# A blocked diagonal scan by quarters, its chunk ends carried in two levels, and output products split by local and entering states

## What is computed

```python
xr = jnp.einsum('btgc,gpc->btgp', uf, bb_re)
xi = jnp.einsum('btgc,gpc->btgp', uf, bb_im)
...
sr, si = complex_scan(jnp.broadcast_to(ar, xr.shape), jnp.broadcast_to(ai, xr.shape), xr, xi)
y = (jnp.einsum('btgp,gcp->btgc', sr, cmat_re) - jnp.einsum('btgp,gcp->btgc', si, cmat_im) + d_skip * uf)
...
mix = (y @ w_glu_v) * jax.nn.sigmoid(y @ w_glu_g)
```

## Time and profile before

| | |
|---|---|
| Median of 3 runs | 2838.79 us (2837.02 to 2840.55) |
| Profiled execution, its own time | 2840.19 us |
| Its span | 2838.5 us |
| TensorE busy | 2742.9 us, 97% |
| VectorE, ScalarE, POOL busy | 1603.1, 1163.9, 388.4 us |
| Mean granted clock | 0.982 of full |

### The profile page before, as it was taken

How to read it: one execution, slowest core, us unless ns; L and a number is a source line. 1 busy time by engine, 2 the same in 40 slices (tenths; PEclk the granted TensorE clock), 3 DMA queues, 4 the chain that set the end, 5 groups by cost and what they waited for, 6 DMA issues and landing times. The chain is left out here.

```text
span 2838.5 us, 53109 instructions
## 1 busy us (share of the span) xinstructions
PE 2742.9 (97%) x19433; PEld 2701.6 (95%) x19433; DVE 1603.1 (56%) x2651; ACT 1163.9 (41%) x1501; POOL 388.4 (14%) x508
## 2 busy tenths in 40 slices
PE   8999999999999999999999993999999999999997
PEld 7999999999999999999999983999999999999996
DVE  7656666555554455655555557665554555455554
ACT  5444445333433333435553332544433344334432
POOL 1333333221000000060002450210000000000011
PEclk9999999999999999999999997999999999999998
DMA  6444444456554545445444420545555554555543
GB/s 176 121 129 122 128 135 123 122 141 156 142 142 141 144 142 146 134 135 147 140 135 136 135 84 5 141 132 154 148 143 150 151 148 142 146 154 149 145 138 95
DMA packets 739209, 382.91 MB, mean 135 GB/s; under 512 B 13560, under 2 KB 734756, under 8 KB 739140
## 3 DMA queue, kind: packets, MB, share of 16 engines
q1 hardware_dynamic: 722352, 365.34, 45.4%
q10 hardware_dynamic: 14228, 9.31, 1.1%
q0 software_dynamic: 2560, 7.29, 1.0%
HBM read 373.31 MB, written 8.57 MB: 135 GB/s over the span
## 5 line engine op out<-in xcount | busy, mean ns | idle before, releaser
L973 DVE TENSOR_TENSOR wl<-raw,wh 128x1024 fp32r<-128x1024 f32 x708 | 894.3, 1264 | 925.4 <-ACT wh L477 924.8
L1499 PE MATMUL banks<-h,wh 128*128 128x336 f32 (+1 forms) x3648 | 1164.6, 319 | 9.2 <-DVE h L983 3.6
L1500 PE MATMUL banks<-h,wh 128*128 128x336 f32 (+1 forms) x3648 | 1152.1, 316 | 0.0
L1501 PE MATMUL banks<-h,wl 128*128 128x336 f32 (+1 forms) x3648 | 1149.7, 315 | 0.0
L477 ACT ACTIVATE wh<-raw 128x1024 fp32r<-128x1024 f32 x708 | 748.8, 1058 | 941.8 <-PE banks L1501 928.4
L1499 PEld LDWEIGHTS banks<-h,wh 128*128 128x128 f32 x3648 | 689.6, 189 | 14.0 <-issue 4.1
L1500 PEld LDWEIGHTS banks<-h,wh 128*128 128x128 f32 x3648 | 689.1, 189 | 3.3 <-issue 1.7
L1501 PEld LDWEIGHTS banks<-h,wl 128*128 128x128 f32 x3648 | 688.6, 189 | 0.0
L1499 PE MATMUL banks<-act,wh 128*128 128x336 f32 (+1 forms) x1888 | 598.6, 317 | 8.6 <-DVE GA L1073 3.2
L1500 PE MATMUL banks<-act,wh 128*128 128x336 f32 (+1 forms) x1888 | 594.7, 315 | 0.0
L1501 PE MATMUL banks<-act,wl 128*128 128x336 f32 (+1 forms) x1888 | 592.8, 314 | 0.0
(11 more groups left out here) (341 smaller groups left out, 1728.3 us busy)
## 6 DMA issues: line engine op xcount, KB each, us to landing
raw<-in_w_up SPq DMA_DIRECT2D x172, 512.0 KB, 4.0
raw<-in_w_gate SPq DMA_DIRECT2D x172, 512.0 KB, 3.9
raw<-in_w_down SPq DMA_DIRECT2D x160, 448.0 KB, 3.6
raw<-in_w_in_e SPq DMA_DIRECT2D x96, 512.0 KB, 3.8
raw<-in_w_out_e SPq DMA_DIRECT2D x32, 512.0 KB, 3.8
raw<-in_w_down SPq DMA_DIRECT2D x32, 512.0 KB, 3.8
raw<-in_w_in_c SPq DMA_DIRECT2D x16, 512.0 KB, 4.1
raw<-in_w_glu_v SPq DMA_DIRECT2D x16, 512.0 KB, 3.8
```

Source lines behind the costliest of these rows:

```text
L973: v.tensor_tensor(wl[:, j % RING, :], raw[:, j % RING, :], wh[:, j % RING, :].bitcast(F32), ALU.subtract) \
L1499: pe.matmul(out, whi, hi, start=first and k == 0, stop=False)
L1500: pe.matmul(out, whi, lo, start=False, stop=False)
L1501: ins = pe.matmul(out, wlo, hi, start=False, stop=last and k == kn - 1)
```

## The change

POOL makes `CT3` before the scan, in what was the table `BX`, and for `CT4` only the zeros; VectorE makes `CT4`. ScalarE takes all eight X products. The scan goes by quarters. The chunk ends are carried within four groups of four chunks at once, then from group to group with the 64th power (`A64`), and a fix-up adds what enters each group, into a tile `SCt` with the chunks innermost. The spread no longer adds into `xs` but writes a ring `sp5`; the output products are made twice, of the local states (75 columns, as quarters are scanned) and of what enters (64 columns). The final states are turned behind the fourth `glu` body. The core of the diff:

```diff
@@ -58,10 +58,10 @@
 CREDIT = 4
...
-POWERS = (1, 2, 3, 4, 8, 12, 16)
+POWERS = (1, 2, 3, 4, 8, 12, 16, 32, 48)
 
 
 COL = {}
...
-            for j in (0, 2, 4, 5, 6, 7):
+            for j in range(8):
                 e.wait_ge(x5, j + 1)
                 take_x(lambda to, x: sc.activation(to, x, ACT.Copy), j).then_inc(x5a, 1)
-            e.wait_ge(scan5, 2)
+            e.wait_ge(scan5, 4)
             sc.activation(fin5[:, 1:1 + NS].rearrange("p s r q -> p r q s"), xs[:, :, :, XW - NS:XW], ACT.Copy)
+            e.wait_ge(quarters, 1)
+            sc.activation(SCt[:, :, :, 0:PCH:4], SC[:, 0:PCH:4].rearrange("p c r q -> p r q c"), ACT.Copy).then_inc(fourth, 1)
+            sc.activation(fin5[:, 0], SC[:, PCH - 1], ACT.Copy).then_inc(fin_made, 1)
...
-                              ACT.Copy).then_inc(ends5, 1)
+                sc.activation(sp5[:, u % SPREAD_RING, :, :, 3, :], SCt[:, :, q, 0:CH], ACT.Copy).then_inc(ends5, 1)
+
+            for u in range(SPREAD_RING):
+                ends(u)
...
+            ph = PH["glu"]
+
+            def glu(i):
+                for j in range(4):
...
+            with e.Fori(0, 4) as i:
+                glu(i)
             for s in range(9):
                 e.wait_ge(fs_t, s + 1)
                 sc.activation(io5o[:, s, :], BM[s % 2][0:2 * PAIRS, 0:P], ACT.Copy).then_inc(fs_c, 1)
...
+            e.wait_ge(out_dma, 16 * (STORES_A + STORES_F + STORES_C))
             ffn(1, None)
...
+            for n, (a5, b5) in enumerate(((0, 0), (1, 0), (1, 1), (3, 3), (4, 3), (4, 4), (6, 6), (7, 6))):
+                pole_product(at(n + 1), at(a5), at(b5))
+            pole_product((A64[:, 1], A64[:, 2]), at(7), at(7))
...
+            e.wait_ge(bx_used, STEP)
+            e.wait_ge(ms_done, 3)
+            for j0 in (0, 4):
+                first, second = (t[:, 0:16 * C5].rearrange("p (q c) -> p q c", c=C5) for t in (sq, ssq))
+                for r in range(2):
+                    times_power(gp, st, C0, 2, r, first, second, OF_C, j0, j0 + 4)
+                    st.then(into_blocks(gp, first, second, CT3[:, j0:j0 + 4, r, :]))
+            gp.memset(sq[:, 0:1], 0.0).then_inc(ct_made, 1)
             e.wait_ge(evac, PH["glu"].group(0, 0) + BANK_CREDIT)
-            gp.tensor_copy(xs[:, :, :, BLK + 1 + PCH:2 * BLK], st5.rearrange("p s r q -> p r q s")).then_inc(st_in, 1)
...
-            for n, to in ((3, CT3), (4, CT4)):
-                gp.memset(to[:], 0.0)
-                for r in range(2):
-                    times_power(gp, st, C0, n - 1, r, cpq[:, r, 0], cpq[:, r, 1], to)
-                for r in range(2):
-                    ins = into_blocks(gp, r, cpq[:, r, 0], cpq[:, r, 1], to)
-                ins.then_inc(ct_made, 1)
-                e.wait_ge(ct_made, n - 2)
+            gp.tensor_copy(xs[:, :, :, BLK + PCH:2 * BLK], st5.rearrange("p s r q -> p r q s")).then_inc(st_in, 1)
+            gp.memset(CT4[:], 0.0).then_inc(ct4_zero, 1)
...
-            e.wait_ge(out_dma, 16 * (STORES_A + STORES_F + STORES_C))
...
+            e.wait_ge(ap_made, 1)
+            for r in range(2):
+                times_power(v, st, C0, 3, r, cpq[:, r, 0], cpq[:, r, 1], OF_C)
+            e.wait_ge(ct4_zero, 1)
+            for r in range(2):
+                ins = into_blocks(v, cpq[:, r, 0], cpq[:, r, 1], CT4[:, :, r, :])
+            ins.then_inc(ct4_made, 1)
...
-            for j in (1, 3):
-                e.wait_ge(x5, j + 1)
-                take_x(v.tensor_copy, j).then_inc(x5v, 1)
...
-            def scan_half(half):
-
...
+
+                v.tensor_tensor(prod0, re, prev, ALU.mult)
+                st.then(v.tensor_tensor(prod1[:, ::-1], ims[:, ::-1], prev, ALU.mult))
+                st.then(v.tensor_tensor(prod0, prod0, prod1, ALU.add))
+
+            def scan_quarter(u):
+
+                q = slice(u * QUARTER, (u + 1) * QUARTER)
+                e.wait_ge(x5a, 2 * u + 2)
                 for i in range(1, 4):
                     n = PCH if i == 1 else PCH + NS
...
-                        e.wait_ge(x5, 8)
...
-            e.wait_ge(st_in, 1)
-            e.wait_ge(x5v, 2)
-            e.wait_ge(x5a, 2)
-            scan_half(0)
-            e.wait_ge(x5a, 6)
-            scan_half(1)
-            with e.Fori(0, PCH - 1) as i:
-                st.enter(i, 3)
-                end = lambda c: SC[:, ds(c, 1)].rearrange("p a r q -> p r (a q)")
-                v.tensor_tensor(cm5[:, 0], AP5[:, 1:2, 6, :].to_broadcast([P, 2, PAIRS]), end(i), ALU.mult)
-                st.then(v.tensor_tensor(cm5[:, 1, ::-1], AP5[:, 0::2, 6, :][:, ::-1], end(i), ALU.mult))
-                st.then(v.tensor_tensor(cm5[:, 0], cm5[:, 0], cm5[:, 1], ALU.add))
-                st.then(v.tensor_tensor(end(i + 1), end(i + 1), cm5[:, 0], ALU.add))
-                st.leave(PCH - 1)
-            v.memset(tiny[:, 11, 6:7], 0.0).then_inc(carried, 1)
...
+                        e.wait_ge(scan5, u + 1)
+
+            for u in range(4):
+                scan_quarter(u)
+
+            e.wait_ge(x5, 8)
+            group = SC[:, 1:PCH].rearrange("p (g m) r q -> p r g m q", m=4)
+            four = [P, 2, 4, PAIRS]
+            for m in range(1, 4):
+                complex_step(g0[:, :, 0], g1[:, :, 0], AP5[:, 1:2, 6, :].unsqueeze(2).to_broadcast(four),
+                             AP5[:, 0::2, 6, :].unsqueeze(2).to_broadcast(four), group[:, :, :, m - 1, :])
+                st.then(v.tensor_tensor(group[:, :, :, m, :], group[:, :, :, m, :], g0[:, :, 0], ALU.add))
+            for g in range(4):
+                complex_step(g0[:, :, 0, 0], g1[:, :, 0, 0], A64[:, 1:2, :].to_broadcast([P, 2, PAIRS]), A64[:, 0::2, :], SC[:, 4 * g])
+                ins = v.tensor_tensor(SC[:, 4 * g + 4], SC[:, 4 * g + 4], g0[:, :, 0, 0], ALU.add)
+                if g < 3:
+                    st.then(ins)
+            ins.then_inc(quarters, 1)
+            e.wait_ge(quarters, 1)
...
+            enters = lambda r: SC[:, 0:CH:4, r, :].unsqueeze(1).to_broadcast(full)
+            by = lambda plane: AP5[:, plane, 6:9, :].unsqueeze(2).to_broadcast(full)
+            for r in range(2):
+                v.tensor_tensor(g0[:, r], by(1), enters(r), ALU.mult)
+                ins = v.tensor_tensor(g1[:, r], by(2 * r), enters(1 - r), ALU.mult)
+            st.then(ins)
+            flat = lambda t: t.rearrange("p r m g q -> p (r m g q)")
+            st.then(v.tensor_tensor(flat(g0), flat(g0), flat(g1), ALU.add))
+            for r in range(2):
+                ins = v.tensor_tensor(SCt[:, r, :, 1:PCH].rearrange("p q (g m) -> p m g q", m=4)[:, 0:3],
+                                      SC[:, 1:PCH, r, :].rearrange("p (g m) q -> p m g q", m=4)[:, 0:3], g0[:, r], ALU.add)
+            ins.then_inc(carried, 1)
+            e.wait_ge(carried, 1)
+            e.wait_ge(fourth, 1)
+            e.wait_ge(kconv, 1)
...
+                S = lambda r: SCt[:, r, q, 0:CH].unsqueeze(2).to_broadcast(full)
+                A = lambda plane: AP5[:, plane, 3:6, q].rearrange("p i q -> p q i").unsqueeze(3).to_broadcast(full)
                 for r in range(2):
-                    S = lambda k: SC[:, 0:CH, k, q].unsqueeze(1).to_broadcast(full)
-                    A = lambda plane: AP5[:, plane, 3:6, q].unsqueeze(2).to_broadcast(full)
-                    v.tensor_tensor(sp5[:, r, 0], A(1), S(r), ALU.mult)
-                    ins = v.tensor_tensor(sp5[:, r, 1], A(2 * r), S(1 - r), ALU.mult)
+                    v.tensor_tensor(slot[:, r, :, 0:3, :], A(1), S(r), ALU.mult)
+                    ins = v.tensor_tensor(sq5[:, r], A(2 * r), S(1 - r), ALU.mult)
...
-                for r in range(2):
-                    ins = v.tensor_tensor(sp5[:, r, 0], sp5[:, r, 0], sp5[:, r, 1], ALU.add)
-                st.then(ins)
-                for r in range(2):
-                    to = xs[:, r, q, 0:3 * BLK].rearrange("p q (i x) -> p i x q", x=BLK)[:, :, 2:2 + CH, :]
-                    ins = v.tensor_tensor(to, to, sp5[:, r, 0], ALU.add)
-                ins.then_inc(spread5, 1)
+                both = slot[:, :, :, 0:3, :].rearrange("p r q i c -> p (r q) i c")
+                v.tensor_tensor(both, both, sq5.rearrange("p r q i c -> p (r q) i c"), ALU.add).then_inc(spread5, 1)
+                e.wait_ge(spread5, u + 1)
...
-            e.wait_ge(evac, PH["glu"].group(0, 0) + BANK_CREDIT)
+            e.wait_ge(evac, PH["glu"].group(0, 0) + BANK_CREDIT - 2)
...
             for j in range(8):
-                if j == 2 or j in (4, 5, 6, 7):
-                    e.wait_ge(x5a, {2: 1, 4: 2, 5: 2, 6: 3, 7: 4}[j])
-                if j in (3, 5):
-                    e.wait_ge(x5v, j // 2)
+                if j == 1:
+                    e.wait_ge(evac, PH["glu"].group(0, 0) + BANK_CREDIT)
+                if j >= 2:
+                    e.wait_ge(x5a, j - 1)
...
-            e.wait_ge(ct_made, 2)
...
+            ins.then_inc(kconv, 1)
...
+            e.wait_ge(ct_made, 1)
+            e.wait_ge(ct4_made, 1)
+            for k in range(8):
+                if k % 2 == 0:
```

(15 more changed lines are left out.)

156 lines of the change are left out of this document (81 added, 75 removed).

## The result

The changed kernel takes 2823.75 us (median of 5, 2817.73 to 2825.56) against 2838.79 us (median of 5 here): ratio 0.9948, 95% interval 0.9935 to 0.9962. That is 15.0 us less; forecast were 2823.2 us and 15.6 us. The profiled execution took 2823.75 us, its span is 2822.0 us.

A forecast was written before the change was run, and what follows sets the result against it. TensorE, busy 97% of the span, was taken as the bound, so only its idle or lower-clock time could pay. Gains of 24.3 us less losses of 8.7 gave 15.6 us net: 2823.2 us, range 2817 to 2829.5.

The forecast's parts named there:

- Scan: VectorE's scan: with POOL's reads gone it runs at the quiet rate, 26.0 us against 31.2, gain 5.2 us.
- the formula: Price of a VectorE scan instruction: 1.055 ns per element and 0.145 us fixed.
- Start of the scan: Head of the scan: starts at 1688.2 us instead of 1689.34, CT3 done early on POOL; gain 1.1 us.
- rival B: Head of the scan: POOL's reads and VectorE's steps hold each other, start 5.8 us later, total 2829.0 us; chance 0.11.
- Carry: Carry of chunk ends on VectorE: two levels and fix-up take 13.3 us against 22.8, gain 9.5 us.
- Spread: Four spreads before the GLU phase: 3.0 us each, 13.2 us against 19.83 with act splits, gain 6.6 us.
- rival D: Spread stage: TensorE at its lower clock bounds it, 11 us more, total 2834 us; chance 0.04.
- The transposes: Final states' nine transposes, moved from ahead of the GLU phase to behind its fourth body: gain 1.9 us in front.
- stall: Behind the fourth GLU body: TensorE waits for ScalarE's queued copies, a new loss of 7.4 us, paid once.
- clock: After the new wait behind the fourth GLU body, TensorE restarts at its lower clock: loss 1.3 us.
- Rival A: Behind the fourth GLU body: no new wait, TensorE finishes the transposes while ScalarE still works; total 2814.5 us; chance 0.08.
- last quarter: From last spread to last act split, ahead of the GLU phase: stays 4.8 us, no gain or loss.

The follow-up runs named there:

- experiment 2: Changed kernel with extra POOL work behind its CT4 memset: thirty two-input multiplies, 2838.67 us (ratio 1.0010), or sixty memsets, 2824.13 us (ratio 0.9953).
- experiment 3: Kernel before with the sixteen turns of the carry written out instead of looped, nothing else changed: 2830.18 us, ratio 0.9976.
- experiment 4: Changed kernel with the products of the local states issued behind the spread instead of during the scan: 2839.82 us, ratio 1.0009.

## Why the prediction was right, and where it was not

**Scan.** Right in mechanism and size: -4.9 for -5.2 us, and both halves of the reason are shown by the multiplies and the memsets (experiment 2). The quarters themselves cost 3.8 us of scan by the fixed cost of a step, as the formula had it.

**Start of the scan.** The step that failed: "It is done at about 1678.5 us, before the last U is there", with 10 us for CT3. It took 13.8 us: 1.5 more because its multiplies and adds cost more than the halves taken for them (0.62 and 0.76 us each), and 2.3 more because POOL's reads and VectorE's two-input instructions lengthen each other. The memset behind it became what VectorE waited for. The term is +0.2 us in this profile, +1.4 in five others and +1.6 in a sixth, not -1.1. That is rival B's mechanism at a quarter to less than half of rival B's price: its 5.8 us assumed that VectorE is held up from end to end, but it collides in four multiplies and one split and then waits.

**Carry.** -9.5 us, as forecast, but the reason was incomplete: 8.2 of it is the loop, 1.3 the two levels (experiment 3).

**Spread.** -7.1 for -6.6: spreads of 3.0 us each, TensorE keeps up, rival D is out. The last 128 products of 64 columns took 2.1 us, so fewer columns do pay within one block of instructions. By the rule of the Trainium skill that was weighed in the prediction (TensorE: Matmul & The Clock Gate, "Back-to-back issue gap", some 25 ns a matmul up to 64 columns) they would have taken 3.2; the trace has 16 ns in a run and 27.6 ns over many blocks (experiment 4), so the figure is passed in a short run, and over a long one the mean stays above it. These products go in turn to four parts of the array of 32 columns each; whether that is what lets them pass it, no run here shows. That the products of the local states are free is right only where they stand; moved behind the spread they cost 16 us of the stretch.

**The transposes.** Gain 1.6 for 1.9, stall 8.4 for 7.4, clock 1.5 and more for 1.3. The mechanism is right, also in its cause (ScalarE's order). The stall was mis-sized because I took the copies' pace, 3.0 us, and the few tenths of the four transposes behind them from stretches at the full clock for the most part; here TensorE turned both at the lower clock, 0.4 us more for each. Rival A is refuted.

**The sum.** By the stages the change is worth 12.1 us in these two profiles, 3.5 less than the forecast: start 1.3, scan 0.3, transposes 0.3, stall 1.0 and what is behind it 1.6 against me, spreads 0.5 and last quarter 0.6 for me. The last of these against me, 1.6, is no more than the scatter of that stretch. By the medians it is 15.0 us, with an interval of 10.8 to 18.4 (0.38 to 0.65% of 2838.8) that holds both. So the forecast's sum came out within 0.6 us of the median partly by luck; its terms are off by 3.5 us on balance.

## What to carry to other kernels

Price a loop with waits inside by comparing the stage's length with the engine's busy time in it: the difference is what unrolling gives, before any better algorithm is thought of. When work is moved behind a bound engine's back, look at which in-order queue it joins and what stands ahead of it there; a few small transposes that wait for ScalarE cost TensorE 8 us and its clock, while the same transposes without waits in an idle microsecond cost nothing, and the clock stayed up behind them in all four executions. An engine that is taken out of a collision at one place should be followed to where its work went: part of it collided again at the head.

## What the runs showed of the hardware

- A long run of unrolled short matmuls took 27.6 ns a matmul with its weight load (64 and 75 columns), with a break of 1.3 to 1.6 us every 128 of them and one 16 KB packet of instructions in each period, although 128 of them pass in 2.10 us, 16 ns each.
- POOL's two-input instructions that read from SBUF suffer too, not only VectorE's: a multiply of 256 elements took 1.49 us beside a weight split and 0.62 alone. Memsets beside VectorE cost it nothing (26.38 us of scan with, 26.35 without).
- With 1.17 us of transposes in TensorE's idle time, the next 14 matmuls ran at a granted clock of 1.00 in four executions of four; without them in one of six. A start at 0.50 cost 1.2 us.
